# W_down of a decoder layer by seven products a block, over a K span that rolls on

## What is computed

```python
def sq_relu_mlp(x, g, w_up, w_down):
    h = rms_norm(x, g) @ w_up
    return jnp.square(jax.nn.relu(h)) @ w_down
...
hp = hp + sq_relu_mlp(hp, mlp_norm[i], w_up[i], w_down[i])
hs = hs + sq_relu_mlp(hs, mlp_norm[i], w_up[i], w_down[i])
```

## Time and profile before

| | us |
|---|---|
| median of 3 runs (2255.12 to 2263.93) | 2260.63 |
| the profiled execution | 2260.23 |
| its span, first to last instruction | 2258.6 |
| mean granted TensorE clock | 0.993 of full speed |
| PE / DVE / ACT busy, share of the span | 97% / 55% / 37% |

### The profile page before, as it was taken

One profiled execution on the slowest core, in us unless ns is written; L12 is line 12 of the kernel. 1 busy time (PEld: TensorE's weight loads), 2 busy tenths in 40 slices (PEclk: granted clock), 3 DMA queues, 4 the chain that ended last, 5 costly groups with the idle time before them and its releaser, 6 DMA issues.

```text
span 2258.6 us, 42813 instructions
## 1 busy us (share of the span) xinstructions
PE 2186.7 (97%) x17481; PEld 2131.8 (94%) x17481; DVE 1233.0 (55%) x1905; ACT 836.6 (37%) x1495; POOL 205.1 (9%) x241
## 2 busy tenths in 40 slices
PE   6999998998899999999999999999999999999998
PEld 5999996676899999999999999999999999999998
DVE  5456666555433787777777777733333343333331
ACT  4233333555322455555555555512212221221212
POOL 5310002443101310000000000000000000000000
PEclk9999999999999999999999999999999999999999
DMA  4333225872333154454454454544333333334223
GB/s 129 92 87 92 84 80 177 266 237 78 94 86 91 48 134 114 122 141 114 121 141 113 122 141 113 163 141 131 94 115 111 104 114 102 123 94 122 84 85 97
DMA packets 420200, 265.45 MB, mean 118 GB/s; under 512 B 19376, under 2 KB 389552, under 8 KB 420096
## 3 DMA queue, kind: packets, MB, share of 16 engines
q1 hardware_dynamic: 417760, 263.06, 40.1%
q0 software_dynamic: 2336, 1.05, 0.3%
...
## 4 chain that ended last, share of the span: by engine, by line
PE 89%; DVE 4%; ACT 2%; SPq 2%; issue 1%; POOL 1%; DMA 1%; POOLq 0%; ACTq 0%; DVEq 0%
PE ps L1686 18%; PE ps L1687 18%; PE ps L1690 18%; PE ps L1965 10%; PE ps L1968 9%; PE ps L1967 9%; PE ps L1810 1%; PE ps L1834 1%; POOL tmp_c L686 1%; PE ps L1881 1%; PE ps L1863 1%; PE ps L1821 1%; PE ps L1848 1%; ACT sprob L878 0%; SPq L425 0%
## 5 line engine op out<-in xcount | busy, mean ns | idle before, releaser
L1141 DVE TENSOR_TENSOR w_lo<-w_raw,w_hi 128x1024 fp32r<-128x1024 f32 x210 | 258.4, 1230 | 691.6 <-ACT w_hi L763 691.3
L1686 PE MATMUL ps<-u_lo,w_hi 128*128 128x272 f32 x2048 | 556.3, 289 | 3.1 <-DVE w_lo L1141 3.1
L1687 PE MATMUL ps<-u_hi,w_hi 128*128 128x272 f32 x2048 | 553.9, 288 | 0.0
L763 ACT CAST w_hi<-w_raw 128x1024 fp32r<-128x1024 f32 x210 | 219.9, 1047 | 869.4 <-PE ps L1690 865.6
L1690 PE MATMUL ps<-u_hi,w_lo 128*128 128x272 f32 x2048 | 425.6, 289 | 0.0
L1686 PEld LDWEIGHTS ps<-u_lo,w_hi 128*128 128x128 f32 x2048 | 386.9, 189 | 3.4 <-issue 3.3
L1687 PEld LDWEIGHTS ps<-u_hi,w_hi 128*128 128x128 f32 x2048 | 385.2, 188 | 0.0
L1686 PE MATMUL ps<-act_lo,w_hi 128*128 128x272 f32 x1312 | 359.8, 291 | 10.6 <-DVE w_lo L1141 8.5
L1687 PE MATMUL ps<-act_hi,w_hi 128*128 128x272 f32 x1312 | 357.0, 290 | 0.0
L1690 PEld LDWEIGHTS ps<-u_hi,w_lo 128*128 128x128 f32 x2048 | 320.2, 188 | 0.0
L1690 PE MATMUL ps<-act_hi,w_lo 128*128 128x272 f32 x1312 | 274.2, 290 | 0.0
...
## 6 DMA issues: line engine op xcount, KB each, us to landing
w_raw<-in_w_up SPq DMA_DIRECT2D x128, 512.0 KB, 5.9
w_raw<-in_w_down SPq DMA_DIRECT2D x128, 512.0 KB, 3.8
w_raw<-in_w_qkv SPq DMA_DIRECT2D x48, 512.0 KB, 3.7
u_rows<-t_buf SPq DMA_DIRECT2D x128, 136.0 KB, 2.3
u_raw<-u_rows SPq DMA_DIRECT2D x32, 544.0 KB, 4.7
w_raw<-in_w_o SPq DMA_DIRECT2D x32, 512.0 KB, 3.8
...
```

Of the source, the lines that this page charges most:

```text
L763: nc.scalar.copy(w_hi[:, k % 2], w_raw[:, k % 4]).then_inc(w_hi_made, 1)
L1141: nc.vector.tensor_tensor(w_lo[:, k % 2], w_raw[:, k % 4], w_hi[:, k % 2], ALU.subtract).then_inc(w_lo_made, 1)
L1686: pe.matmul(out[:, a, :], wh, l[:, cols], start=start, stop=False)
L1687: pe.matmul(out[:, a, :], wh, h[:, cols], start=False, stop=False)
```

## The change

- W_down is also done by seven products. There are 32 visits v; a visit makes two output tiles for both token halves (row pair v mod 8) over eight pairs of chunks, v to v+7 modulo 32, so each output pair is visited four times and sees all 32 pairs. The products of a visit are D1 D7 D6 D2 D5 D4 D3; weights enter as four slots of 512 KB as in W_up, with sums s3, s2, s1, s4 on DVE. A visit has 7 x 8 x 3 = 168 matmuls; two tiles over two blocks of eight chunks had 192.
- The seven input sums of u are made as its quads come out: `input_sums` on DVE forms four more rows of 272, and SP stores seven rows of 136 KB a quad instead of four. The relus and squares of a quad move ahead, and input_sums stands before the last product's remainders.
- d_raw and d_fac hold the seven operands for eight pairs, where W_up's operands lay (d_raw is the lo half of the same place). At the change-over `load_operand(n)` fills one operand when the last quad has used what lay there; `operand_cast` and `operand_rest` cut it in two halves. From visit 1 on only the pair that rolled in is loaded, cast and cut, in two parts: early (three operands, D1, D7, D6), fetched once the visit before has done D6, and late (four operands), fetched when it has ended.
- A visit's results are added to xT in several steps: `take_a` in the visit, `take_bd`, `take_wf` (two additions) and `take_zx` in the next; copies a, f, b, d to c_buf on ACT let PE go on adding in the same PSUM bank.
- y is turned in the last eight visits, two chunks a visit, one visit behind; only two chunks are left after the last.
- PE's W_down loops are written out instead of being loops of the engine. In visits 25 to 31 a weight slot comes by two DMAs, since the span wraps.

```diff
+        d_raw = [at("d_raw0", [P, 3, 2, UC, HALF], F32, kq_at)[0], at("d_raw1", [P, 4, 2, UC, HALF], F32, act_at)[0]]
+        d_fac = [at("d_fac0", [P, 3, 2, UC, HALF], F32R, kq_at)[0], at("d_fac1", [P, 4, 2, UC, HALF], F32R, act_at)[0]]
+        y_buf = [at("y_buf0", [P, TT, P], F32, tmp_c_at)[0], at("y_buf1", [P, TT, P], F32, t_buf_at)[0]]
...
-        u_rows = nc.dram_tensor("u_rows", [DFF // P, P, T], F32).ap()
+        u_rows = nc.dram_tensor("u_rows", [DFF // P // 2, P, 7, HALF], F32).ap()
...
-        w_down_v = w_down[0].rearrange("(k p) n -> p k n", p=P)
+        w_down_v = w_down[0].rearrange("(k e p) n -> p e k n", p=P, e=2)
...
+        NV = DFF // P // 2
+        RND = KC // 2
+        A_END = QH * NQ
+        D1, D7, D6, D2, D5, D4, D3 = range(7)
+        ADD_A, ADD_BD, ADD_W, ADD_F, ADD_ZX = range(5)
+        U_T1, U_N4, U_B21, U_B22, U_B11, U_T2, U_T3 = range(7)
+        PART = [U_B11, U_T3, U_T2, U_B21, U_T1, U_N4, U_B22]
+        OPS = [slice(U_B11, U_T3 + 1), slice(U_T1, U_B22 + 1)]
...
+            def store_sums(q):
+                sp.wait_ge(a_t, 4 * q + 4)
+                sp.dma_start(u_rows[q, :, U_T1, :], t1_row).then_inc(u_stored[U_T1], 16)
+                sp.dma_start(u_rows[q, :, U_T2, :], t2_row).then_inc(u_stored[U_T2], 16)
+                sp.dma_start(u_rows[q, :, U_T3, :], t_buf[:, C12]).then_inc(u_stored[U_T3], 16)
+                sp.dma_start(u_rows[q, :, U_N4, :], n4_row[:]).then_inc(u_stored[U_N4], 16)
...
+            def load_operand(n):
+
+                sp.wait_ge(a_used, QH * (NQ - 1) + 2 * n + 2)
+                part = PART[n]
+                sp.wait_ge(u_stored[part], 16 * UC)
+                sp.dma_start(part_of(d_raw, part)[:, 1], u_rows[0:UC, :, part, :].rearrange("k p t -> p k t")
+                             ).then_inc(u_loaded[n], 16)
+
+            def load_pair(v, late):
+
+                pair = (v - 1 + UC) % NV
+                ops = OPS[late]
+                sp.wait_ge(a_used, A_END + QH * (v - 1) + (QH if late else 2 * D6 + 2))
+                for part in range(ops.start, ops.stop):
+                    sp.wait_ge(u_stored[part], 16 * (pair + 1))
+                sp.dma_start(d_raw[late][:, :, 1, (v - 1) % UC, :], u_rows[pair, :, ops, :]).then_inc(pair_loaded[late], 16)
...
             for q in range(NQ):
                 if q:
-                    store_u(q - 1, C11)
+                    store_row(q - 1, C11, U_B11)
...
+                    for a in (A11, A21, A22):
                         load_factor(q + 1, a)
...
+                    if q:
+                        store_row(q - 1, C22, U_B22)
+                        store_row(q - 1, C21, U_B21)
+                    load_factor(q + 1, A12)
+                    if q:
+                        store_sums(q - 1)
+            load_operand(0)
+            load_down(0, A11)
+            load_down(0, A21)
+            load_operand(1)
+            load_down(0, A22)
+            store_row(NQ - 2, C22, U_B22)
+            store_row(NQ - 2, C21, U_B21)
+            load_operand(2)
+            load_down(0, A12)
+            load_operand(3)
+            load_operand(4)
+            load_operand(5)
+            store_sums(NQ - 2)
+            load_operand(6)
+
...
+            for v in range(NV):
+                last = v - (NV - RND) - 1
+                if last >= 1:
+                    store_y(2 * last - 1, 2 * last - 1)
+                if v + 1 < NV:
+                    for a in (A11, A21, A12):
+                        load_down(v + 1, a)
+                    load_pair(v + 1, 0)
+                    load_down(v + 1, A22)
...
+                if last >= 0:
+                    store_y(2 * last, 2 * last)
+                if v + 1 < NV:
+                    load_pair(v + 1, 1)
+                if v == 1:
+                    store_row(NQ - 1, C11, U_B11)
+                    store_row(NQ - 1, C22, U_B22)
+                    store_row(NQ - 1, C21, U_B21)
+                    store_sums(NQ - 1)
...
+            def pair_cast(v, late):
+
+                act.wait_ge(pair_loaded[late], 16 * v)
+                r = (v - 1) % UC
+                nc.scalar.copy(d_fac[late][:, :, 0, r, :], d_raw[late][:, :, 1, r, :]).then_inc(u_hi_made, 1)
...
+            def cast_down(v, n, h):
+
+                g = QH * v + 2 * n + h
+                if g < 4:
+                    act.wait_ge(a_used, QH * NQ + g - 3)
+                else:
+                    act.wait_ge(a_used, A_END + g - 3)
...
+            def copy_f(v):
+                act.wait_ge(a_used, A_END + QH * v + 2 * D7 + 2)
+                if v:
+                    act.wait_ge(y_add, added(v - 1, ADD_F))
+                else:
+                    act.wait_ge(a_add, 4 * (NQ - 1) + 3)
+                nc.scalar.copy(c_buf[:, 1], down_bank(v, 2)).then_inc(a_copy, 1)
...
-                for n in range(7, 10):
-                    cast(q, n)
+                cast(q, 7)
                 if q == 1:
                     square_u(0, C11)
+                for i in (C12, C22, C21):
+                    square_u(q - 1, i)
+                cast(q, 8)
+                cast(q, 9)
                 take_x(q, 1)
-                for n in range(10, 13):
-                    cast(q, n)
...
+                if q == NQ - 1:
+                    operand_cast(0, 0)
+                    operand_cast(0, 1)
+                cast(q, 12)
                 take_x(q, 2)
                 cast(q, 13)
...
+            operand_cast(1, 0)
+            operand_cast(1, 1)
+
...
+            for v in range(NV):
+                last = v - (NV - RND) - 1
+                cast_down(v, D1, 0)
+                if v == 0:
+                    operand_cast(2, 0)
+                cast_down(v, D1, 1)
+                if v == 0:
+                    operand_cast(2, 1)
+                if last >= 1:
+                    take_y(2 * last - 1, 2 * last - 1)
+                cast_down(v, D7, 0)
+                if v == 0:
+                    take_x(NQ - 1, 3)
+                cast_down(v, D7, 1)
+                if v == 0:
+                    operand_cast(3, 0)
+                    operand_cast(3, 1)
+                cast_down(v, D6, 0)
+                copy_a(v)
+                cast_down(v, D6, 1)
+                if v == 0:
+                    operand_cast(4, 0)
+                    operand_cast(4, 1)
                 else:
...
+                    pair_cast(v, 1)
+                cast_down(v, D2, 0)
+                cast_down(v, D2, 1)
+                if v == 0:
+                    operand_cast(5, 0)
+                    operand_cast(5, 1)
+                copy_f(v)
+                cast_down(v, D5, 0)
+                copy_b(v)
+                cast_down(v, D5, 1)
+                if v == 0:
+                    operand_cast(6, 0)
+                    operand_cast(6, 1)
+                if v == 1:
+                    for i in (C11, C12, C22, C21):
+                        square_u(NQ - 1, i)
+                cast_down(v, D4, 0)
+                cast_down(v, D4, 1)
+                if last >= 0:
+                    take_y(2 * last, 2 * last)
+                if v + 1 < NV:
+                    pair_cast(v + 1, 0)
+                cast_down(v, D3, 0)
+                copy_d(v)
+                cast_down(v, D3, 1)
...
-                    dve.wait_ge(u_stored[i], 16 * q)
+                    dve.wait_ge(a_t, 4 * q)
+                    dve.wait_ge(u_stored[(U_B11, U_T3, U_B22, U_B21)[i]], 16 * q)
...
+            def input_sums(q):
+
+                dve.wait_ge(a_sq, 4 * q + 4)
...
+                nc.vector.tensor_tensor(t1_row, t_buf[:, C12], t_buf[:, C11], ALU.subtract).then_inc(a_t, 1)
+                dve.wait_ge(a_t, 4 * q + 1)
...
+                nc.vector.tensor_tensor(t2_row, t_buf[:, C22], t1_row, ALU.subtract).then_inc(a_t, 1)
+                nc.vector.tensor_tensor(t_buf[:, C12], t_buf[:, C12], t_buf[:, C22], ALU.subtract).then_inc(a_t, 1)
+                dve.wait_ge(a_t, 4 * q + 3)
...
+                nc.vector.tensor_tensor(n4_row[:], t_buf[:, C21], t2_row, ALU.subtract).then_inc(a_t, 1)
...
+            def pair_rest(v, late):
+
+                dve.wait_ge(u_hi_made, 14 + 2 * (v - 1) + late + 1)
+                r = (v - 1) % UC
+                nc.vector.tensor_tensor(d_fac[late][:, :, 1, r, :], d_raw[late][:, :, 1, r, :], d_fac[late][:, :, 0, r, :],
+                                        ALU.subtract).then_inc(u_lo_made, 1)
...
+            def take_wf(v):
+                _, row2 = down_rows(v)
+                dve.wait_ge(y_add, added(v, ADD_BD))
+                dve.wait_ge(a_used, A_END + QH * v + 2 * D4 + 2)
+                nc.vector.tensor_tensor(row2[:, 0:HALF], row2[:, 0:HALF], down_bank(v, 2), ALU.add).then_inc(y_add, 1)
+                nc.vector.tensor_tensor(row2[:, HALF:T], row2[:, HALF:T], c_buf[:, 1], ALU.add).then_inc(y_add, 1)
...
+                for i in (C12, C22, C21):
+                    relu(q - 1, i)
...
+                sum4(q)
```

(97 more changed lines are left out.)

352 lines of the change are left out of this document (186 added, 166 removed).

## The result

| | us |
|---|---|
| median before, measured beside it | 2259.43 (2255.12 to 2263.93) |
| median of the changed kernel | 2178.7 (2177.0 to 2179.36) |
| ratio | 0.9641, 95% interval 0.9621 to 0.9662 |
| forecast, and its range | 2174 (2164 to 2192) |
| profiled execution of the changed kernel, its span | 2178.64, 2177.1 |

The change takes 81 us off, 5 fewer than forecast. The span was forecast at 2172.2 (2173.8 less 1.6 around it).

What follows compares the result with a forecast made beforehand. TensorE, busy 97% of the span, was taken to bound the kernel. Matmuls removed 96.8, change-over -13.3, tail +2.9 make 86.4 us off 2260.2: forecast 2174 us, range 2164 to 2192.

Steps and rivals of the forecast that it cites:

- Matmuls: W_down: 128 tiles at 774.9 us become 32 visits at 678.1 us, 96.8 us gone if PE stays fed.
- Steady visits: W_down visits: DVE 17.5 and ACT 11.5 of 21.19 us both fit, no stall taken.
- the two tight runs: Two stretches of a visit's half products: 5.8 of 6.06 us and 8.8 of 9.08 us, slack 0.3 us.
- rival 1: Steady visits lose the tight run, 0.3 to 1.0 us in 31 visits: 2183 to 2205 us; chance 0.18.
- Late pair: Rolled pair's second load, issued at a visit's end: lands in 3.8 to 4.7 us, needed by 5.8, so hidden.
- rival 5: Rolled pair lands late, each us over 5.8 lost in each of 31 visits: 2273 us at 9.0; chance 0.03.
- W_up: W_up quads: added DVE work makes 18.2 of 21.19 us, stores land in 2.3 us, cost nothing.
- The change-over: Between W_up and W_down: 12.0 + 5.0 + 0.7 - 4.4 = 13.3 us worse than before.
- the 12.0: Change-over: DVE's chain of operand remainders and other work makes D4 start 12.0 us late, at 48.3 instead of 36.3.
- the 5.0: Change-over, visit 0: DVE's addition waits 5.0 us more for row T3's store, queued on SP behind loads.
- rival 3: Low clock holds through visit 0, which ends about 5 us later: 2179 us; chance 0.07.
- The tail: After the last matmul: 6.4 us, with 8.7 us of turns among the last seven visits; gain 2.9 us.

Runs made afterwards that it cites:

- experiment 4: Changed kernel with each visit's early pair load issued ahead of the next visit's A12 load on SyncE: 2176.22 us, ratio 0.9638.
- experiment 5: Changed kernel with each visit's late pair load issued behind the next visit's A11 and A21 loads instead of ahead: 2427.9 us, ratio 1.0745.
- experiment 6: Experiment 1's kernel with SyncE's change-over loads in the order in which their places come free: 2170.72 us, ratio 0.9604.
- runs 1, 9 and 10: Experiment 1, experiment 10, and between them first operands' remainders cut to 8 of 272 columns on top of experiment 6: 2165.18 us.
- run 3: Experiment 1's kernel with the first operands' remainders cut to 8 of 272 columns a chunk, matmuls kept: 2168.32 us, ratio 0.9599.
- run 11: Experiment 10's kernel with the first operands' remainders cut to 8 of 272 columns a chunk, matmuls kept: 2161.06 us, ratio 0.9565.
- experiment 2: Changed kernel with only quad 30's row T3 store moved from SyncE's queue to ScalarE's: 2171.26 us, ratio 0.9613.
- experiment 1: Changed kernel with quad 30's four sum stores issued on SyncE ahead of operands 3 to 5: 2173.18 us, ratio 0.9617.
- experiment 10: Experiment 6 plus experiment 4, with operand 0's casts earlier, three additions later and the last quad's relus, squares, sums and stores spread over visits: 2163.77 us.

## Why the prediction was right, point by point

The time, the direction and the mechanism hold; the 4.9 us that the span missed are in terms that can be named.

**Matmuls.** A W_up quad repeats after 21.19 us as before; a visit without a wait takes 21.25, not 21.19. Over the 30 visits between the copies of visits 1 and 31 that is 1.7 us. Each visit has seven waits for a pair that a quad hasn't; that these are the 0.06 was not tried.

**Steady visits: the step that failed, by 3.1 us.** I took no stall. VectorE is busy 17.2 us where 17.5 were worked out, and the two tight runs held. (ScalarE is busy 10.3; the prediction's 11.5 is a slip of addition, its terms make 10.5.) But ten visits are 0.05 to 0.7 us longer, 3.1 us together. I priced the late pair and let the early one pass, though its load stands on SyncE behind A12's, which waits for a sum of the running visit: it took 5.2 us from issue to landing (3.4 in experiment 4) and was issued too late. The two pairs on the page of the changed kernel (count, KB, us to landing), late pair first:

```profile
d_raw<-u_rows SPq DMA_DIRECT2D x31, 544.0 KB, 3.9
...
d_raw<-u_rows SPq DMA_DIRECT2D x31, 408.0 KB, 5.2
```

VectorE stood about 2 us a visit for it, and what slack was left was sometimes too little. This is rival 1 by another door, with a loss of 0.1 a visit instead of 0.3 to 1.0.

**Late pair.** It lands in 3.9 us (3.8 to 4.7 taken) and costs nothing; experiment 5 bears out rival 5, one for one from 6.1 us on (5.8 in the prediction).

**W_up.** VectorE 18.10 (18.2 worked out), quads unchanged: no cost. The 2.3 us for a store were too few: with seven stores a quad the page's median is 4.4, and the additions came late enough all the same (they waited once, 0.3 us, between 800 and 1440 us).

**The change-over.** Predicted 12.0 + 5.0 = 17.0, measured 18.8. The chain holds in detail: a remainder of 1088 steps by 1.20, PE stood 2.01 ahead of P3 (2.4 predicted) and VectorE 4.74 for T3's store (5.0), and without that wait 4.4 us went. PE's gaps make 12.3 us (12 to 20 forecast). The 1.8 more come mainly from two waits of VectorE for ScalarE (0.60 and 1.58 us), which itself stood 4.08 and 2.67 us for operands 1 and 2 to land: the step that I left out. With the loads in order (experiment 6) both waits are gone, VectorE waits 0.80 us for the store, and the excess is 12.5: 11.7 without that, for the 12.0 of the sum. What the sum couldn't say is what the 12.0 are worth: with the remainders cut, 4.6, 5.3 and 3.5 us came back in three settings, not 12, as operands and casts are late next. These gains are good to some 2 us, since the clock differs too: it is at 0.50 in one stretch of the change-over in runs 1, 9 and 10, in two in run 6, in a longer one in run 3 and in none in run 11, and one such stretch cost some 1.5 us (13 matmuls, 1.6 us at full rate, took 3.1 in the changed kernel). The rule of ring order that I cited beside the 5.0 (the Trainium skill, DMA: Bandwidth & Descriptors, section Queues, rings and completion order) is borne out: on SyncE's queue row T1 landed at 1476.4, 0.4 us behind operand 5, and T3 0.8 behind T1, while on a queue of its own T3 passed operand 5 (experiment 2).

**Low clock.** It went to 0.50 behind P3's gap in the last quad (1458.3 to 1461.6) and twice in visit 0, not through all of it (rival 3). By the chain it cost little of its own, since PE waited for VectorE again behind each: ahead of D4 it stands 0.65 us both here and in experiment 1, where the clock stays at 1.00 through visit 0 and the excess falls by no more than VectorE's wait. No run changes the clock alone. Rival 3's row, a gap of 2.31 us that left the clock at 1.00, doesn't carry over: in the changed kernel the gap at the same place, 2.31 us too, took it to 0.50 (window 779.0 to 782.3).

**Visit 1 and the turns of y.** Visit 1: 0.9 over 21.25 (0.7 predicted); experiment 10 takes it away. A visit with two turns is 1.05 longer, not 1.24: 1.1 us gained over six visits.

**The tail.** The last rows (compare); 5.8 us follow the end of the last W_down matmul (2171.3), 6.4 predicted, and the second turn waits for the copies of the first as said.

```profile
2171.13 0.71 PE L2305 MATMUL ps<-ident,xT 128*128 128x128 f32 x5
...
2172.75 0.74 PE L2305 MATMUL ps<-ident,xT 128*128 128x128 f32 x5 [0.91 <-ACT y_buf L1223]
...
2174.55 0.50 SPq L688 DMA_DIRECT2D out<-y_buf  x1
```

**The sum of the misses**: change-over +1.8, visits' base +1.7, longer visits +3.1, visit 1 +0.2, turns -1.1 and -0.2 in the last visit, tail -0.6, and the last quad began 0.3 earlier: 4.6 of the 4.9. That the miss is so small is in part luck: 6.8 too little and 2.2 too much.
